# Cross attention of the sample tile: values weighted by probabilities held as 32-column weights, and the last norm rows in another order

## The reference

```python
def cross_and_ffn(h, mk, mv, w_xq_l, w_xo_l, g2, b2, w_up_l, w_down_l, g3, b3):
    q = (h @ w_xq_l).reshape(B, T, X_HEADS, X_HEAD_DIM)              # 4 heads of 128
    s = jnp.einsum('bthd,bmhd->bhtm', q, mk) * (X_HEAD_DIM ** -0.5)  # m: 256 memory tokens
    p = jax.nn.softmax(s, axis=-1)
    o = jnp.einsum('bhtm,bmhd->bthd', p, mv).reshape(B, T, X_WIDTH)
    h = layer_norm(DN_ALPHA * h + o @ w_xo_l, g2, b2)
    ...
```

## Time and profile before

| | us |
|---|---|
| median of 3 executions | 4292.5 (4289.44 to 4299.41) |
| the profiled execution | 4295.71 |
| its span in the trace | 4293.5 |
| `values(8)` in the two layers, first matmul | 1276.65 and 3406.46 |
| last `hcopy` of the block, end | 1329.12 and 3458.94 |

### The profile page before, as it was taken

The page is one execution under the profiler, slowest core; times in us unless marked ns, Lnnn a source line. Parts: engine busy times, 40 slices in busy tenths (PEclk is TensorE's granted clock), DMA queues, the critical chain, the costliest instruction groups (busy, mean ns, idle before and its releaser), DMA issues. The chain is left out here.

```text
span 4293.5 us, 50474 instructions
## 1 busy us (share of the span) xinstructions
PE 3882.1 (90%) x19162; PEld 2689.9 (63%) x19162; DVE 2055.1 (48%) x4141; ACT 977.0 (23%) x1922; POOL 1180.3 (27%) x1047
## 2 busy tenths in 40 slices
PE   6899987889997999999879998878899979999996
PEld 4344564444566998889643445644445668888985
DVE  5799555432144333333567994554221343333335
ACT  2201224421122122111231012344111222111222
POOL 3014672223022212112330156632130231212213
PEclk8899957999997999999979999589999889999998
DMA  3111003460211111111020110044501111111111
GB/s 139 41 43 47 6 1 104 146 231 0 79 35 64 39 57 41 39 39 39 10 95 28 39 43 6 2 158 148 174 23 56 40 67 51 39 39 39 47 41 42
DMA packets 143022, 254.97 MB, mean 59 GB/s; under 512 B 24577, under 2 KB 76162, under 8 KB 142594
## 3 DMA queue, kind: packets, MB, share of 16 engines
q1 hardware_dynamic: 130562, 215.00, 14.6%
q0 software_dynamic: 12288, 37.76, 2.6%
HBM read 231.31 MB, written 21.42 MB: 59 GB/s over the span
## 5 line engine op out<-in xcount | busy, mean ns | idle before, releaser
L2357 PE MATMUL ps<-ffn_parts 128*128 128x512 f32 (+1 forms) x3456 | 801.8, 391 | 7.4 <-DVE arena L2487 7.4
L2347 PE MATMUL ps<-ffn_parts 128*128 128x384 f32 (+1 forms) x4608 | 779.7, 330 | 25.9 <-POOL ffn_parts L2432 25.9
L2347 PEld LDWEIGHTS ps<-ffn_parts 128*128 128x128 f32 x4608 | 775.3, 189 | 31.2 <-POOL ffn_parts L2432 26.9
L2357 PEld LDWEIGHTS ps<-ffn_parts 128*128 128x128 f32 (+1 forms) x3456 | 623.4, 182 | 174.7 <-DVE arena L2487 24.2
L2487 DVE TENSOR_TENSOR arena<-arena,ps 128x1024 f32<-128x1024 f32 (+1 forms) x288 | 351.2, 1219 | 342.5 <-PE ps L2357 338.4
L889 PE MATMUL ps<-arena,arena_rest 128*128 128x512 f32 (+1 forms) x1152 | 379.5, 492 | 3.7 <-PEq L445 2.7
L2437 POOL TENSOR_TENSOR ffn_parts<-arena,ffn_parts 128x1024 fp32r<-128x1024 f32 x64 | 154.2, 2409 | 611.3 <-ACT ffn_parts L2391 611.3
L899 PE MATMUL ps<-arena_rest,arena 128*128 128x512 f32 (+3 forms) x864 | 318.7, 526 | 2.3 <-ACT arena_rest L1072 2.3
L889 PEld LDWEIGHTS ps<-arena,arena_rest 128*128 128x128 f32 x1152 | 191.8, 193 | 193.5 <-issue 192.1
L322 DVE TENSOR_SCALAR_CACHE_REDUCE arena_rest<-arena_rest,small 128x384 bf16<-128x384 f32 (+4 forms) x330 | 278.8, 875 | 2.1
L1941 PE MATMUL ps<-arena_rest,arena 128*128 128x512 f32 (+1 forms) x576 | 254.4, 601 | 22.0 <-DMA arena_rest<-in_w_out 22.0
(11 more groups left out here) (291 smaller groups left out, 5036.2 us busy)
## 6 DMA issues: line engine op xcount, KB each, us to landing
arena_rest<-in_kv SPq DMA_DIRECT2D x128, 256.0 KB, 9.4
arena<-in_w_down SPq DMA_DIRECT2D x32, 1024.0 KB, 7.6
arena_rest<-in_w_in SPq DMA_DIRECT2D x10, 2048.0 KB, 8.1
ffn_raw<-in_w_up SPq DMA_DIRECT2D x16, 1024.0 KB, 5.8
arena<-in_w_up SPq DMA_DIRECT2D x16, 1024.0 KB, 5.9
out_y_prompt<-arena SPq DMA_DIRECT2D x3, 4096.0 KB, 15.9
arena<-out_y_prompt SPq DMA_DIRECT2D x2, 4096.0 KB, 24.7
arena_rest<-in_mem_kT SPq DMA_DIRECT2D x16, 512.0 KB, 7.2
```

The costliest lines, as they stand in the source:

```text
L2347: ins = pe.matmul(bank(3 * c + b, y - x), w[:, k, :], h[:, k, x:y], start=(k == 0 and h is HH and w is WH), stop=(k == KC - 1 and w is WL))
L2357: ins = pe.matmul(bank(b0 + a)[0:R, :], u[:, c, tcol(t)], d[:, c, 512 * a:512 * a + 512], start=(c == 0 and u is UH and d is DH), stop=(c ...
```

## The change

`values(8)` swaps its operands. The probabilities are copied from PSUM into PB8, ordered so that one sample's 4 heads x 8 tokens are 32 adjacent columns; these are the weights, and all 512 columns of the sample's values move through. Four samples go to the four groups of 32 columns of the array and so to the four quarters of a PSUM bank, two halves of the memory are summed, and two groups of four samples fill banks 0 and 1: 16 matmuls. The result has for each row (sample, head, token) all four heads' dimensions, of which one is wanted. So each bank is copied to SBUF (OG), turned by 4 transposes, and `pick` copies the wanted blocks to OT, two heads by ScalarE and two by VectorE. All 8 samples' values now have buffers: samples 4 to 7 use the key buffers SK, and are loaded when all sample scores are done.

Besides, VectorE does `ln.unit_rows(7)` ahead of its part of the picks and so ahead of the residual sum of tile 8, and it does tile 8's gain and bias itself; GpSimd stops after tile 7. The turn of tile 8 waits for VectorE's new semaphore.

```diff
+    SV += [x.rearrange("p h m -> p (h m)").rearrange("p (a n) -> p a n", a=2) for x in SK]
+    PB8 = at(RR, r0 + 8192, 2, DB, XH * DT)
+    OG = Pb[:, 1, :].rearrange("p (g n) -> p g n", g=2)
+
+    def pick(h):
+        src = ps[:, 1024:2048].rearrange("p (g h j r q) -> p g h j r q", g=2, h=XH, j=4, r=XH)[:, :, h, :, h, :]
+        return OT[:, h, 0:NS].rearrange("p (g j q) -> p g j q", g=2, j=4), src
...
+            sp.wait_ge(s_sb, DB)
             for b in range(4, DB):
-                sp.wait_ge(s_vb, b - 3)
                 values_in(b)
...
+                    pe.wait_ge(s_ex, NT)
+                    for g in range(2):
+                        for j in range(4):
+                            pe.wait_ge(s_sv[j], 16 * (g + 1))
+                        for a in range(2):
+                            for j in range(4):
+                                b = 4 * g + j
+                                ins = pe.matmul(bank(g)[32 * j:32 * j + 32, :],
+                                                PB8[:, a, b, :],
+                                                SV[b][:, a, :], start=(a == 0), stop=(a == 1), skip_group_check=True)
+                        ins.then_inc(s_gv, 1)
+                    for g in range(2):
+                        pe.wait_ge(s_ge, g + 1)
                         for h in range(XH):
-                            for a in range(2):
-                                ins = pe.matmul(bank(4)[:, h * P + b * DT:h * P + (b + 1) * DT],
-                                                SV[b % 4][:, a, h * P:(h + 1) * P],
-                                                PT[:, 2 * h + a, b * DT:(b + 1) * DT], start=(a == 0), stop=(a == 1))
-                        ins.then_inc(s_vb, 1)
+                            ins = pe.transpose(bank(2 + g)[:, h * P:(h + 1) * P], OG[:, g, h * P:(h + 1) * P], ident)
+                    ins.then_inc(s_gt, 1)
...
             def project(t):
+                    pe.wait_ge(s_pe, t + 2)
+                    pe.wait_ge(s_gc, 2)
...
+                        for a in range(2):
+                            act.copy(PB8[:, a].rearrange("p b (h q) -> p h b q", h=XH), ...).then_inc(s_te, 1)
...
+                        for g in range(2):
+                            act.wait_ge(s_gv, g + 1)
+                            act.copy(OG[:, g, :], bank(g)).then_inc(s_ge, 1)
                         act.wait_ge(s_xp, t)
+                        act.wait_ge(s_gt, 1)
+                        for h in range(2):
+                            act.copy(*pick(h)).then_inc(s_pe, 1)
...
-            for t in range(NT):
+            for t in range(NT - 1):
                 ln.pool(ch, pool, t)
...
+                if t == NT:
+                    ln.unit_rows(ch, dve, t - 2)
+                    dve.wait_ge(s_gt, 1)
+                    for h in range(2, XH):
+                        dve.tensor_copy(*pick(h)).then_inc(s_gc, 1)
...
+            x = X[0:NS, NT - 1, :]
+            dve.wait_ge(ln.in_, 32)
+            dve.wait_ge(ln.unit, NT)
+            ch(dve.tensor_tensor(x, x, ln.g[0:NS], ALU.mult))
+            dve.tensor_tensor(x, x, ln.b[0:NS], ALU.add).then_inc(s_l8, 1)
```

More of the change, by code:

```diff
@@ L2049, in values_in @@
             def values_in(b):
-                sp.dma_start(SV[b % 4], lay(i["mem_v"], layer)[:, b].rearrange("l (a p) d -> p (l a) d", p=P)
+                sp.dma_start(SV[b], lay(i["mem_v"], layer)[:, b].rearrange("l (a p) d -> p (l a) d", p=P)
                              ).then_inc(s_sv[b % 4], 16)
@@ L2097, in turn @@
                 R = rows(t)
-                pe.wait_ge(ln.ready, t + 1)
+                if t < NT - 1:
+                    pe.wait_ge(ln.ready, t + 1)
+                else:
+                    pe.wait_ge(s_l8, 1)
                 for half in range(2):
@@ L2118, in values @@
             def values(t):
-                pe.wait_ge(s_te, t + 1)
+                pe.wait_ge(s_te, t + 1 if t < NT - 1 else t + 2)
                 if t:
@@ L2128, in values @@
                 else:
-                    for b in range(DB):
-                        pe.wait_ge(s_sv[b % 4], 16 * (b // 4 + 1))
-                        for h in range(XH):
-                            for a in range(2):
-                                ins = pe.matmul(bank(4)[:, h * P + b * DT:h * P + (b + 1) * DT],
-                                                SV[b % 4][:, a, h * P:(h + 1) * P],
-                                                PT[:, 2 * h + a, b * DT:(b + 1) * DT], start=(a == 0), stop=(a == 1))
-                        ins.then_inc(s_vb, 1)
+                    pe.wait_ge(s_ex, NT)
[11 more added lines that the diff above has]
+                        pe.wait_ge(s_ge, g + 1)
+                        for h in range(XH):
+                            ins = pe.transpose(bank(2 + g)[:, h * P:(h + 1) * P], OG[:, g, h * P:(h + 1) * P], ident)
+                    ins.then_inc(s_gt, 1)
             def project(t):
                 R = rows(t)
-                pe.wait_ge(s_pe, t + 1)
+                if t < NT - 1:
+                    pe.wait_ge(s_pe, t + 1)
+                else:
+                    pe.wait_ge(s_pe, t + 2)
+                    pe.wait_ge(s_gc, 2)
                 if t == 0:
@@ L2198, in _ @@
                         act.wait_ge(s_pv, t)
-                    act.copy(PT[:, :, 0:R], ps[:, 1024:2048].rearrange("p (n s) -> p n s", n=8)[:, :, 0:R]
-                             ).then_inc(s_te, 1)
+                    if t < NT - 1:
+                        act.copy(PT, ps[:, 1024:2048].rearrange("p (n s) -> p n s", n=8)).then_inc(s_te, 1)
+                    else:
+                        for a in range(2):
+                            act.copy(PB8[:, a].rearrange("p b (h q) -> p h b q", h=XH),
+                                     ps[:, 1024:2048].rearrange("p (h a b q) -> p h a b q", h=XH, a=2, q=DT
+                                                                )[:, :, a, 0:DB, :]).then_inc(s_te, 1)
                     if t < NT - 1:
                         act.wait_ge(s_pv, t + 1)
-                    else:
-                        act.wait_ge(s_vb, DB)
-                    if t:
+                        if t:
+                            act.wait_ge(s_xp, t)
+                        act.copy(OT[:, :, 0:R], bank(4).rearrange("p (h s) -> p h s", h=XH)[:, :, 0:R]
+                                 ).then_inc(s_pe, 1)
+                    else:
+                        for g in range(2):
+                            act.wait_ge(s_gv, g + 1)
+                            act.copy(OG[:, g, :], bank(g)).then_inc(s_ge, 1)
                         act.wait_ge(s_xp, t)
-                    act.copy(OT[:, :, 0:R], bank(4).rearrange("p (h s) -> p h s", h=XH)[:, :, 0:R]).then_inc(s_pe, 1)
+                        act.wait_ge(s_gt, 1)
+                        for h in range(2):
+                            act.copy(*pick(h)).then_inc(s_pe, 1)
                 if 2 <= t < NT + 2:
@@ L2263, in _ @@
                     ln.stats(ch, dve, t - 1)
-                if t >= 2:
+                if t >= 2 and t != NT:
                     ln.unit_rows(ch, dve, t - 2)
+            x = X[0:NS, NT - 1, :]
[3 more added lines that the diff above has]
+            dve.tensor_tensor(x, x, ln.b[0:NS], ALU.add).then_inc(s_l8, 1)
             keep(e, ch, "dve")
```

6 lines of the change are left out of this document (4 added, 2 removed).

## The result

| | us |
|---|---|
| median before, four executions in the same session | 4294.2 (4289.4 to 4299.4) |
| median of the change, four executions | 4246.0 (4242.2 to 4248.6) |
| ratio | 0.9888, 95% interval 0.9874 to 0.9902 |
| profiled execution of the change, and its span | 4248.6, 4246.7 |

The change is 48 us faster; 4248 was forecast, with 4242 to 4261 as the range. A second session, at the end, gave 4249.6 against 4293.1 (ratio 0.9897, 0.9880 to 0.9913), 43.5 us.

A forecast was written before the change was run, and what follows sets the result against it. TensorE, busy 90% of the span, was taken as the bound, idling or slow-clocked at the end of cross attention; 15.5 + 6.8 = 22.3 us per layer, 44.6 in two, gives a median of 4248 us, range 4242 to 4261.

The forecast's parts named there:

- The sum: In `values(8)`: four column groups run side by side, so 3.7 us at full clock replaces 23.8.
- The way back: From value sum to OT: copy to OG, transposes and hand-over to 5.1 us, ScalarE's picks, `ln.act(6)` at 5.5.
- The queue ahead of `project(8)`: VectorE's picks behind `unit_rows(7)`, done at 10.5: `project(8)` starts 11.0 us after the first value matmul, 15.5 gained.
- `project(8)`: Last projection: keeps 16 records, clock low at its start, 9.4 us; bounds 7.0 and 13.9.
- The tail: From the end of `project(8)` to the last copy: 9.8 us instead of 16.6, 6.8 gained.
- Loads: Values of samples 4 to 7: issued 19.4 us before the first value matmul, hidden, worth nothing.
- The total: End of the cross-attention block: 15.5 + 6.8 = 22.3 us gained per layer, 44.6 in two layers.
- the clock low throughout: Rival: clock stays low over all of `project(8)`, 4.5 us more per layer, 4257 us; chance 0.10.
- the late picks: Rival: `unit_rows(7)` waits for both GpSimd instructions, ending at 13.0 instead of 10.5, 4253 us; chance 0.05.
- no overlap: Rival: column groups of the value sum do not overlap, 14 us instead of 3.7, 4269 us; chance 0.02.
- no change: Rival: the value sum's 32 records in line at half clock, 0.87 us each, 4297 us; chance 0.03.

The follow-up runs named there:

- e8: The changed kernel with all 16 value matmuls in column group 0 and the first quarter of each bank: sum 13.9 us, 4272.9 us, one execution.
- e6: The changed kernel with four more dense matmuls, result unused, ahead of `project(8)`: `project(8)` lasts 7.05 us, 4245.4 us, one execution.
- e2: The kernel before plus only the norm rows (early `unit_rows(7)`, tile 8's gain and bias on VectorE): 4279.6 us, ratio 0.9967.
- e7: e4 with `unit_rows(7)` behind the residual sum of tile 8 again, gain and bias still on VectorE: 4247.2 us, one execution.
- e1: The change with the norm rows put back as before, so only the value swap remains: 4249.3 us, ratio 0.9899 to the kernel before.
- e3: The changed kernel with both memory halves of a sample one after the other, order alone changed: sum 3.68 us, 4251.4 us, one execution.
- e4: The changed kernel with all four picks by ScalarE, none by VectorE: 4238.1 us, ratio 0.9868 to the kernel before.
- e5: e4 with `project(8)` ahead of `turn(5)`, and roots of tiles 7 and 8 ahead of `hcopy(5)` and `hcopy(6)`: 4236.0 us, ratio 0.9862.
- e9: e5 with ScalarE doing the roots of tiles 6 and 7 among the OG copies: 4237.1 us, ratio 0.9870 to the kernel before.

## Why the prediction was right

- **The sum.** 3.7 forecast, 3.64 measured, at full clock. The earlier trace rows carried it: same form, 8 records in 1.06. The measured end is near the lower bound of 3.5 to 4.0, so change of shape costs little. The Trainium skill (TensorE: Matmul & The Clock Gate, Packing small matmuls) has the gain of 3.07 from which the prediction worked out 4.6, for four row groups. It did not hold for the four column groups here: e8 over the change is 13.92/3.64 = 3.8. The prediction did not split the 20 gained in the sum; by e8 10.3 is overlap and 9.9 the clock.
- **The way back.** Picks at 5.1, `ln.act(6)` at 5.3 (5.5 forecast): two picks take 0.33, not 0.52. (The terms 3.7, 0.59 and 0.69 give 5.0, where the prediction wrote 5.1; its 5.5 goes by 5.0.)
- **The queue ahead of `project(8)`.** 10.7 against 11.0. VectorE's `unit_rows(7)` ended 0.54 behind GpSimd's first instruction, as in the one row of before (0.55), so VectorE got its turn between two of GpSimd's. The Trainium skill (SBUF — State Buffer, Who interferes with whom) has one engine hold the shared port pair for its whole instruction; 1.64, 2.33 and 3.17 in these traces agree. One step ahead of it was off and did not show: from `ln.act(6)` to the end of `ln.act(7)` it took 2.6 (1283.66 to 1286.25), not the 3.4 read where the transposes in between ran at the lower clock. `unit_rows(7)` so began its big instruction at 8.7 instead of 9.6, and only the wait for GpSimd brought its end back to 10.3, near the 10.5 forecast.
- **`project(8)`.** 9.4 forecast, 8.75 measured, low for 4 us instead of 5: the term that was mis-sized, by 0.6. The place where the clock fell was right, and so was its tie to the lack of dense work, as far as e6 shows it.
- **The tail.** 9.8 forecast, 9.88 measured; e2 shows that it is shortened by the norm rows alone, and e7 that moving gain and bias without `unit_rows(7)` would not do: its tail is 15.5.
- **Loads.** Hidden, 19 us ahead, as forecast.
- **The total.** 22.3 per layer forecast, 23.2 measured. What the prediction did not see: that the two gains (15.5 and 6.8) have a price that one puts on the other. It walked through VectorE's queue and so had the right time, but credited the norm rows with 6.8, of which 2.1 is left over e1. And it took the wait for `unit_rows(7)` as given, where two copies on another engine end it.

Of the rivals, the clock low throughout, the late picks, no overlap and no change did not come; e8 shows what no overlap would have cost, 10.25 per layer (10.3 forecast).

## What to carry to other kernels

When few columns move past many weights, swap the operands, and if the weights are then 32 columns wide, spread them over the four column groups: here 23.8 became 3.64. Half of that, 10.3, is overlap. The other half is the clock, which fell under the old matmuls and not under the new; at one clock the swap without the overlap would have gained nothing (13.9 against an estimated 13.5), so look at the clock before you credit the shape. When an engine's small copy releases the bottleneck engine, look at what stands ahead of it in its queue; here 0.34 us of copies waited 3.6 us behind norm rows that nobody needed yet, and the gap cost clock as well. And measure the parts of a change one by one: 21.1 and 8.4 made 23.2.

## What the runs showed of the hardware

- The order of records over the column groups doesn't matter within 0.04 us (e3, 3.68 against 3.64), which I had not expected: TensorE fills all four groups even when four records in a row go to one.
- At a granted clock of 1.00 a record with 128 columns of weights and 8 moving columns took 0.105, one with 32 columns of weights and 512 moving columns 0.43 (before, e8). The clock fell to 0.52 after some 3 us of the first kind and stayed at 1.00 over 13.9 us of the second.
- The granted clock was still 1.00 over 7.0 us with 2.3 us of transposes, and 0.57 in the 4 us behind them, when dense work had begun again. With dense work in the last 3.7 us of that gap it stayed at 1.00 (e6), and with `project(8)` begun 3 us earlier as well (e1, e4). In rows of transposes with waits of 0.8 us at most between them it fell in e5 and still stood at 1.00 at the same distance in e9; what decides between the two stays open.
- A tensor-tensor instruction of VectorE on SBUF, 1.22 alone, took 3.17 when it began inside one of GpSimd's (e7). `unit_rows`'s 128x1024 instruction, 0.81 alone, took 1.64 for the same reason, and GpSimd's next took 2.67 in place of 2.34 (the change).
